# Hybrid decoder step on one core: the pooling, S5-gate and up-projection stages of the kernel written as one stage

## The chip, the core and the metric

The kernel runs on one core of a Trainium2 chip. The number that counts is the time of one execution in microseconds (us), as the device reports it; a kernel's figure is the median of its runs. The engines are TensorE (PE, its weight loads PEld), VectorE (DVE), ScalarE (ACT), GpSimd (POOL) and SyncE (SP, which here only starts transfers).

## The reference

One layer of a decoder trunk over 1024 prompt rows and 64 sample rows (1088 columns of work, `NT`). After RMSNorm and one input projection, three branches run side by side and are merged. What the change touches is the end of the layer:

```python
# S5 branch: y is the state-space output, w_glu is 512 x 512
y = jax.nn.gelu(y.reshape(bt, t, S5_W))
y = y * jax.nn.sigmoid(y @ w_glu)
# pooling branch: trailing means over 2, 4, 8, 16 rows, one 128-channel group each
outs.append((end - beg) / cnt)
pooled = jnp.concatenate(outs, axis=-1) - uf
mixed = jnp.einsum('btgc,gcd->btgd', pooled, pool_w) * pool_scale
# every branch: SiLU gate path, projection 512 -> 1024, sigmoid merge gate
u_s5 = (y_s5 * jax.nn.silu(s5_z)) @ w_up_s5
u_rw = (y_rw * jax.nn.silu(rw_z)) @ w_up_rwkv
u_pl = (y_pl * jax.nn.silu(pl_z)) @ w_up_pool
merged = gates[:, :, 0] * u_s5 + gates[:, :, 1] * u_rw + gates[:, :, 2] * u_pl
out = merged @ w_o
x = x + rmsnorm(out, g_post)
```

The last rows of the branches (shift row, pooling rows, RWKV state) are outputs too.

## The kernel before

All data are float32. A product that must be exact to float32 is made of three fp32r products (`split_mm`, lines 311 to 313): each operand is split into a high part (an ACT copy) and a low part (operand minus high part, on POOL or DVE). `CH` cuts the 1088 columns into chunks of 384, 384 and 320; `WB` = 4 is the number of 128-channel blocks of a branch, `KT` = 8 that of the model width. Activations lie as channels by columns. The order of work on each engine is the order in which its block of the program is written, and engines wait for one another by semaphores. Between two stages all engines meet at a barrier. All transfers are started by SP, in its program order.

Earlier stages (norm, input projection, RWKV) leave the projected columns in a DRAM tensor `projected`, the RWKV result in `y_branches`, and the S5 output in `s5_y_chunks`. Then come four stages:

- **Pooling** (`phase_pool`): SP loads all four pooling blocks, the tails and the pooling gate. PE turns the tails round (transposes, L1811 to L1824), ACT copies them out (L1839 to L1845), SP stores them. DVE makes doubling sums over all blocks at once (L1885, L1886), a pooled block per window (L1889 to L1894); PE multiplies it by a 128x128 weight in plain float32 (L1834), DVE scales and gates it (L1877). The result goes to DRAM (`y_branches`, L1803), and the stage ends when it has landed.
- **S5 gate** (`phase_glu`): SP loads the S5 output in eight pieces of 16 partitions (L1943), then the gate weight and the S5 gate path (L1944, L1945), then, for RWKV and pooling, a block's branch output and gate path (L1938, L1940) through three buffers. ACT does GELU (L2002) and SiLU (L2006), PE 48 plain float32 products (L2039), ACT their sigmoids (L2019). The table `order` (L1928) puts RWKV and pooling blocks ahead of and between the S5 blocks: SiLU (L2012), product on DVE (L1956), high part on ACT (L1999), low part on POOL (L1984).
- **Up projections** (`phase_up`): 24 units, for each of eight output blocks the three branches in turn; a unit is 36 fp32r matmuls over three chunks, in six PSUM banks. Per unit SP loads a weight and a merge gate (two buffers each), ACT splits the weight (L2087) and takes the gate's sigmoid (L2089), POOL makes the weight's low part (L2112), DVE multiplies a chunk by its gate and adds it to one accumulator (L2151, L2156). After every third unit the accumulator is split by ACT (L2096) and POOL (L2106) into `merged_hi` and `merged_lo`. The units are a loop of three rounds of six after a first six.
- **Output** (`phase_out`): the `w_o` product, the norm and the residual.

Of the kernel before, what the change touches and what calls it, by code (L numbers as in the profile page):

```python
# [19 lines left out]
ALU = mybir.AluOpType  # L20
# [1737 lines left out]
def phase_pool(nc, io, e):  # L1758

    EX = BUF + SEQ  # L1760
    ES_ = BUF + NS
    with ExitStack() as ctx:
        sem = lambda n: ctx.enter_context(nc.semaphore(n))
        sb = lambda n, s, d=F32: ctx.enter_context(nc.sbuf_tensor(n, s, d))
        ux, usx = sb("pool_ext", [P, WB, EX])[:, :, :], sb("pool_ext_s", [P, WB, NB, ES_])[:, :, :, :]
        fresh = sb("pool_fresh", [P, WB, NB * NS])
        old = sb("pool_old", [NB * BUF, W])
        pw = sb("pool_weights", [P, WB, P])

        sums = [sb(f"pool_sum{i}", [P, WB, EX]) for i in range(2)]  # L1770
        ssums = [sb(f"pool_ssum{i}", [P, WB, NB, ES_]) for i in range(2)]
        inv = sb("pool_inv", [P, WB, BUF])
        pooled = sb("pooled", [P, WB, NT])
        y_pl, z_pl = sb("y_pl", [P, WB, NT]), sb("z_pl", [P, WB, NT])
        z_loaded, z_silu = sem("pl_z_loaded"), sem("pl_z_silu")
        tail = sb("shift_tail", [P, RB, 1 + NB * NS])
        tail9 = sb("shift_cols", [P, RB, 1 + NB])
        shift_rows = sb("shift_rows_new", [1 + NB, RB * P])
        tail_p, tail_s = sb("pool_tail", [P, WB, BUF]), sb("pool_tail_s", [P, WB, NB * BUF])
        rows_p, rows_s = sb("pool_rows", [BUF, W]), sb("pool_rows_s", [NB * BUF, W])  # L1780
        st_rows = sb("rwkv_rows", [HD, H, HD])
        ps = [ctx.enter_context(nc.psum_tensor(f"pool_ps{i}", [P, 512], F32)) for i in range(8)]
        loaded, stored = sem("pl_loaded"), sem("pl_stored")
        flip, tails, done, mm_done, chain = [sem(n) for n in ("pl_flip", "pl_tails", "pooled_done", "pl_mm", "pl_chain")]
        flip2, rows_done, scaled = sem("pl_flip2"), sem("pl_rows"), sem("pl_scaled")
        scr = lambda b0, k, a, b: e.scratch[b0:b0 + k, :, a:b].rearrange("b p t -> p b t")
        with nc.Block() as block:
            @block.sync
            def _(sp):
                sp.dma_start(ux[:, :, BUF:EX], scr(B_PLX, WB, 1, 1 + SEQ)).then_inc(loaded, 16)  # L1790
                sp.dma_start(fresh[:, :, :], scr(B_PLX, WB, 1 + SEQ, 1 + NT)).then_inc(loaded, 16)
                sp.dma_start(old[:, :], io["state_pool"][0].rearrange("b t w -> (b t) w")).then_inc(loaded, 16)
                sp.dma_start(pw[:, :, :], io["pool_w"][0].rearrange("g c d -> c g d")).then_inc(loaded, 16)
                sp.dma_start(tail[:, :, :], scr(B_RW, RB, SEQ, 1 + NT)).then_inc(loaded, 16)
                sp.dma_start(z_pl[:, :, :], scr(B_PLZ, WB, 1, 1 + NT)).then_inc(z_loaded, 16)
                sp.wait_ge(rows_done, 7)
# [5 lines left out]
                sp.wait_ge(scaled, 3 * WB)  # L1802
                sp.dma_start(e.y_scr[2], y_pl[:, :, :]).then_inc(stored, 16)  # L1803
                sp.wait_ge(stored, 16 * 6)

            @block.tensor
            def _(pe):
                pe.wait_ge(loaded, 16 * 5)

                for b in range(WB):  # L1810
                    mm = pe.transpose(ps[0][:, b * NB * BUF:(b + 1) * NB * BUF], old[:, b * P:(b + 1) * P], e.ident[0:NB * BUF, 0:NB * BUF])  # L1811
                mm.then_inc(flip, 1)

                for b in range(WB):
                    mm = pe.transpose(ps[1][0:HD, b * P:(b + 1) * P], e.s_a[:, b, :], e.ident)
                mm.then_inc(flip2, 1)
                pe.wait_ge(tails, 3)
                for r in range(RB):
                    mm = pe.transpose(ps[2 + r // 4][0:1 + NB, (r % 4) * P:(r % 4 + 1) * P], tail9[:, r, :], e.ident)
                mm.then_inc(flip2, 1)  # L1820
                for b in range(WB):
                    mm = pe.transpose(ps[6][0:BUF, b * P:(b + 1) * P], tail_p[:, b, :], e.ident)
                for b in range(WB):
                    mm = pe.transpose(ps[7][0:NB * BUF, b * P:(b + 1) * P], tail_s[:, b, :], e.ident)  # L1824
                mm.then_inc(flip2, 1)
                for g in range(WB):
                    pe.wait_ge(done, g + 1)
                    for c, (at, n) in enumerate(CH):
                        q = g * 3 + c
                        if q == 0:  # L1830
                            pe.wait_ge(rows_done, 7)
                        if q >= 8:
                            pe.wait_ge(scaled, q - 7)
                        pe.matmul(ps[q % 8][:, 0:n], pw[:, g, :], pooled[:, g, at:at + n], start=True, stop=True).then_inc(mm_done, 1)  # L1834

            @block.scalar
            def _(act):
                act.wait_ge(flip2, 1)
                act.activation(st_rows[:, :, :], ps[1][0:HD, :].rearrange("v (h k) -> v h k", k=HD), ACT.Copy).then_inc(rows_done, 1)  # L1839
                act.wait_ge(flip2, 3)  # L1840
                for q in range(4):
                    n = min(4, RB - 4 * q) * P
                    act.activation(shift_rows[:, q * 512:q * 512 + n], ps[2 + q][0:1 + NB, 0:n], ACT.Copy).then_inc(rows_done, 1)
                act.activation(rows_p[:, :], ps[6][0:BUF, :], ACT.Copy).then_inc(rows_done, 1)
                act.activation(rows_s[:, :], ps[7][0:NB * BUF, :], ACT.Copy).then_inc(rows_done, 1)  # L1845
                act.wait_ge(z_loaded, 16)
                for g in range(WB):
                    act.activation(z_pl[:, g, :], z_pl[:, g, :], ACT.Silu).then_inc(z_silu, 1)

            @block.vector  # L1850
            def _(dve):
                ch = Chain(dve, chain)
                tt = dve.tensor_tensor
                ch.after(dve.memset(ux[:, :, 0:BUF], 0.0))

# [6 lines left out]
                dve.wait_ge(loaded, 16 * 5)  # L1862
                dve.tensor_copy(tail9[:, :, :], tail[:, :, 0:1 + NB * NS:NS]).then_inc(tails, 1)
                dve.tensor_copy(tail_p[:, :, :], ux[:, :, SEQ:EX]).then_inc(tails, 1)
                dve.wait_ge(flip, 1)
                ch.after(dve.tensor_copy(usx[:, :, :, 0:BUF], ps[0][:, 0:WB * NB * BUF].rearrange("p (w b t) -> p w b t", w=WB, b=NB)))
# [536 lines left out]
```

## Time and profile before

| | us |
|---|---|
| median of 3 runs (lowest, highest) | 1542.83 (1541.0, 1543.42) |
| profiled execution, its own time | 1539.99 |
| its span, first to last instruction | 1538.3 |
| PE, PEld busy | 1337.4, 1218.6 (87%, 79%) |
| DVE, ACT, POOL busy | 711.5, 480.1, 415.1 |
| mean granted TensorE clock | 0.935 |

The profile is of one execution. The busy sums say that TensorE works through most of the span; the 40 slices of the page show where it does not: in the slices from about 1115 to 1270 us PE is at 2 to 4 tenths, and the granted clock at 6 or 7 tenths of full speed. Those are the pooling and the S5-gate stage. The time outside the span is 1539.99 - 1538.3 = 1.69 us.

### The profile page before, as it was taken

To read this page: it belongs to the slowest core of one execution; us is meant where nothing else is said; L and a number is where in the kernel's file an instruction comes from. 1 tells how busy PE (TensorE), PEld (TensorE's weight loads), DVE (VectorE), ACT (ScalarE), POOL (GpSimd) and SP (SyncE) were. 2 spreads that over 40 slices of the span, in tenths; PEclk is the share of its full clock that TensorE was granted. 3 is DMA by queue.
4 is the path that set the end of the run, shared out by engine and by line. 5 is a ranking of instruction groups with operands and counts; after the bars stand their busy time and mean duration, and the time that the engine had idled before them with its cause. 6 is when DMAs were issued, how large, how long until landed. Compare 5 with 4: busy or idle time off the path is not lost. (4 is left out here: it accounts for less than half of the span.)

```text
span 1538.3 us, 32479 instructions
## 1 busy us (share of the span) xinstructions
PE 1337.4 (87%) x14048; PEld 1218.6 (79%) x14048; DVE 711.5 (46%) x1480; ACT 480.1 (31%) x851; POOL 415.1 (27%) x426
## 2 busy tenths in 40 slices
PE   3898999995799999999999999999823449997897
PEld 3897999995689889999988989899721239997785
DVE  5347724523637372827272737362315254444032
ACT  6121122121325242425252424252102443332221
POOL 6116457451112222222222221211000142332400
PEclk7898999998899999999999999999966679999899
DMA  5341422234222222222222222211063924442432
GB/s 180 78 114 34 120 90 86 69 105 117 51 62 70 76 65 81 65 76 70 76 65 82 64 80 61 70 53 57 21 180 92 231 87 143 142 128 83 146 137 69
DMA packets 158889, 141.33 MB, mean 92 GB/s; under 512 B 32096, under 2 KB 143761, under 8 KB 158625
## 3 DMA queue, kind: packets, MB, share of 16 engines
q1 hardware_dynamic: 158752, 139.33, 31.2%
q8 instruction: 107, 1.75, 0.5%
q14 instruction: 30, 0.24, 0.1%
HBM read 93.56 MB, written 44.57 MB: 90 GB/s over the span
## 5 line engine op out<-in xcount | busy, mean ns | idle before, releaser
L311 PE MATMUL f_ps<-h_hi,fw_hi 128*128 128x384 f32 (+1 forms) x864 | 305.2, 353 | 0.0
L313 PE MATMUL f_ps<-h_hi,fw_lo 128*128 128x384 f32 (+1 forms) x864 | 282.7, 327 | 0.0
L312 PE MATMUL f_ps<-h_lo,fw_hi 128*128 128x384 f32 (+1 forms) x864 | 282.2, 327 | 0.0
L1107 POOL TENSOR_TENSOR fw_lo<-fw,fw_hi 128x1024 fp32r<-128x1024 f32 x36 | 86.4, 2400 | 558.6 <-ACT fw_hi L1142 558.6
L311 PEld LDWEIGHTS f_ps<-h_hi,fw_hi 128*128 128x128 f32 x864 | 162.5, 188 | 13.8 <-issue 4.1
L311 PE MATMUL proj_ps<-h_hi,whi 128*128 128x384 f32 (+1 forms) x504 | 170.9, 339 | 1.1 <-PEq L220 1.1
L312 PE MATMUL proj_ps<-h_lo,whi 128*128 128x384 f32 (+1 forms) x504 | 166.2, 330 | 0.0
L313 PE MATMUL proj_ps<-h_hi,wlo 128*128 128x384 f32 (+1 forms) x504 | 166.1, 330 | 0.0
L312 PEld LDWEIGHTS f_ps<-h_lo,fw_hi 128*128 128x128 f32 x864 | 162.9, 189 | 3.9 <-issue 3.8
L313 PEld LDWEIGHTS f_ps<-h_hi,fw_lo 128*128 128x128 f32 x864 | 162.7, 188 | 0.0
L1186 ACT ACTIVATE f_out<-f_ps 128x384 f32<-128x384 f32 (+1 forms) x108 | 50.8, 470 | 281.4 <-PE f_ps L313 281.4
L311 PE MATMUL up_ps<-branch_hi,up_w_hi 128*128 128x384 f32 (+1 forms) x288 | 95.4, 331 | 23.7 <-PEq L1931 20.5
L1381 DVE TENSOR_TENSOR t_m<-t_m,q 128x256 f32<-128x256 f32 (+1 forms) x66 | 27.6, 418 | 174.1 <-PE q L1539 174.0
L311 PEld LDWEIGHTS proj_ps<-h_hi,whi 128*128 128x128 f32 x504 | 96.3, 191 | 3.4 <-issue 1.7
L312 PEld LDWEIGHTS proj_ps<-h_lo,whi 128*128 128x128 f32 x504 | 96.4, 191 | 0.5
L313 PEld LDWEIGHTS proj_ps<-h_hi,wlo 128*128 128x128 f32 x504 | 96.2, 191 | 0.0
L313 PE MATMUL up_ps<-branch_hi,up_w_lo 128*128 128x384 f32 (+1 forms) x288 | 94.6, 328 | 0.0
L312 PE MATMUL up_ps<-branch_lo,up_w_hi 128*128 128x384 f32 (+1 forms) x288 | 94.5, 328 | 0.0
L311 PEld LDWEIGHTS up_ps<-branch_hi,up_w_hi 128*128 128x128 f32 x288 | 54.6, 189 | 26.0 <-issue 21.0
L678 POOL TENSOR_TENSOR wlo<-wst,whi 128x1024 fp32r<-128x1024 f32 x18 | 43.3, 2406 | 104.7 <-ACT whi L882 104.0
L311 PE MATMUL out_ps<-wo_hi,merged_hi 128*128 128x512 f32 (+1 forms) x144 | 57.5, 399 | 12.9 <-POOL wo_lo L2210 12.2
L1984 POOL TENSOR_TENSOR branch_lo<-up_y,branch_hi 128x1088 fp32r<-128x1088 f32 x8 | 21.4, 2689 | 161.1 <-ACT branch_hi L1999 161.1
(418 smaller groups left out, 2635.9 us busy)
## 6 DMA issues: line engine op xcount, KB each, us to landing
fw<-in_w_in_dram SPq DMA_DIRECT2D x36, 512.0 KB, 4.7
projected<-f_out SPq DMA_DIRECT2D x72, 192.0 KB, 2.0
up_gate<-projected SPq DMA_DIRECT2D x24, 544.0 KB, 3.8
wst<-in_w_in_dram SPq DMA_DIRECT2D x21, 512.0 KB, 5.7
projected<-proj_out SPq DMA_DIRECT2D x17, 544.5 KB, 3.1
raw<-projected SPq DMA_DIRECT2D x8, 838.5 KB, 7.7
projected<-f_out SPq DMA_DIRECT2D x36, 160.0 KB, 2.1
up_y<-y_branches SPq DMA_DIRECT2D x8, 544.0 KB, 4.3
```

The costliest lines, as they stand in the source:

```text
L311: pe.matmul(out, whi, xhi, start=first, stop=False)
L312: pe.matmul(out, whi, xlo, start=False, stop=False)
L313: return pe.matmul(out, wlo, xhi, start=False, stop=last)
L678: pool.tensor_tensor(wlo[:, n % R], wst[:, n % R], whi[:, n % R].bitcast(F32), ALU.subtract).then_inc(lo_done, 1)
L1107: pool.tensor_tensor(wlo[:, r], wst[:, r], whi[:, r].bitcast(F32), ALU.subtract).then_inc(fw_lo, 1)
L1186: act.activation(stage[:, u % 3, 0:n], fps[u % 2][:, 0:n], ACT.Copy).then_inc(f_free, 1)
L1381: tt(tm[rows, hs], tm[rows, hs], q4(TXB[q])[rows], ALU.subtract).then_inc(ev["tmn"], 1)
L1984: pool.tensor_tensor(e.yl[:, br, b], y[:, n % YB], e.yh[:, br, b].bitcast(F32), ALU.subtract).then_inc(lo, 1)
```

## The change

`phase_pool`, `phase_glu` and `phase_up` become one stage, `phase_end`, with no barrier and no DRAM round trip inside.

- The first loads: SP starts the S5 output, RWKV blocks 0 and 1, the first two up weights, the tails and pooling weights, a gate, RWKV blocks 2 and 3, a gate and two pooling blocks; ACT starts the gate weight and the S5 gate path itself, ahead of its first activation.
- The S5 gate goes block by block (m = 0 to 3): three sigmoids, then RWKV block m whole (SiLU, product, high and low part), then copies of the turned tails.
- The 24 units run branch by branch (RWKV, S5, pooling), written out, in four PSUM banks instead of six; the sums of all eight output blocks stay in an SBUF tensor `up_acc`, and each is split for the output stage in the third run (n >= 18).
- Pooling is cut into single blocks and put between units: its sums and pooled blocks on DVE, its 12 products on PE in the other four banks after units 1, 5, 9 and 12, its SiLU and high parts on ACT, its low parts on POOL. It reads 0.5 MB blocks through two buffers and never goes to DRAM.

```diff
-def phase_pool(nc, io, e):
+UPS = [(br, m) for br in (1, 0, 2) for m in range(KT)]
+def phase_end(nc, io, e):
...
+    UB = 4
+        acc = sb("up_acc", [P, KT * NT])
+        aux = ps[4:8]
...
             def _(sp):
+                def load_rwkv(b):
+                    if b >= 2:
+                        sp.wait_ge(r_lo, b - 1)
...
+                def load_gate(n):
+                    br, m = UPS[n]
+                    if n >= 2:
+                        sp.wait_ge(gated, 3 * (n - 1))
...
+                for n in range(2, n_up):
+                    load_w(n)
+                    load_gate(n)
+                    if n in (2, 3):
+                        load_pool_gate(n - 2)
+                    if n in (3, 6):
+                        load_pool(2 + n // 6)
+                    if n in (10, 11):
+                        load_pool_gate(n - 8)
...
             def _(act):
+                act.dma_start(w5[:, :, :], io["s5_w_glu"][0].rearrange("(k p) m -> p k m", p=P)).then_inc(w5_loaded, 16)
+                act.dma_start(u5, scr(B_S5Z, WB, 1, 1 + NT)).then_inc(z5_loaded, 16)
...
+                for m in range(WB):
+                    for c, (_, n) in enumerate(CH):
+                        q = m * 3 + c
+                        act.wait_ge(mm5, q + 1)
+                        if q >= 2:
+                            act.wait_ge(out5, q - 1)
+                        act.activation(gate5[:, q % 2, 0:n], aux[q % UB][:, 0:n], ACT.Sigmoid).then_inc(sig5, 1)
+                    act.wait_ge(yz_loaded[m % 2], 32 * (m // 2 + 1))
+                    act.activation(uz[:, m % 2], uz[:, m % 2], ACT.Silu).then_inc(r_silu, 1)
+                    if m < 2:
+                        split(m)
+                    rwkv_high(m)
+                    if m:
+                        act.wait_ge(flip, m)
+                        for q in ((0, 1, 2), (3, 4, 5), (6,))[m - 1]:
+                            take(q)
...
             def _(pe):
+                for m in range(WB):
+                    glu(m)
+                    if m:
+                        turn_tails(m - 1)
+                for n in range(n_up):
+                    up(n)
+                    if n == 1:
+                        pe.wait_ge(sig5, 12)
+                        pool_products(0)
+                    if n == 5:
+                        pool_products(1)
+                    if n == 9:
+                        pool_products(2)
+                    if n == 12:
+                        pool_products(3)
...
             def _(dve):
+                for n in range(n_up):
+                    if n == 0:
+                        level(0, 0)
+                        pool_block(0)
+                    up(n)
+                    if n == 1:
+                        level(1, 0)
+                        level(1, 1)
+                    if n == 2:
+                        pool_block(1)
+                        level(2, 0)
...
-        phase_pool(nc, io, e)
...
-            phase_glu(nc, io, e)
...
-            phase_up(nc, io, e)
+        phase_end(nc, io, e)
```

Where instructions stand, in program order. First SP's queue from the stage's first transfer (before: from the S5-gate stage; `glu_yc` and the first `end_early` are the S5 output, the pairs from `y_branches` and `projected` are RWKV or pooling blocks):

```order
L1943 DMA glu_yc<-s_y_chunks 16x32x136 x8
L1944 DMA glu_w<-in_s_w_glu_dram 128x4x512
L1945 DMA glu_u<-projected 128x4x1088
L1938 DMA up_y<-y_branches 128x1088
L1940 DMA up_z<-projected 128x1088
```

The same place of the changed kernel, where one tensor `end_early` holds the S5 buffers and the branch buffers:

```order
L1843 DMA end_early<-s_y_chunks 16x32x136 x8
L1818 DMA end_early<-y_branches 128x1088
L1819 DMA end_early<-projected 128x1088
L1818 DMA end_early<-y_branches 128x1088
L1819 DMA end_early<-projected 128x1088
L1834 DMA up_w<-in_w_up_rwkv_dram 128x4x128 x2
L1848 DMA up_acc<-projected 128x13x65
```

The gate weight (1 MB) and the S5 gate path (2.1 MB) have left SP's queue; they are the first two instructions on ACT.

ACT in the kernel before, from the first sigmoid of the S5 gate (`glu_gate`) on; `branch_hi` are the high parts:

```order
L2019 ACT_TABLE_LOAD
L2019 ACTIVATE glu_gate<-glu_ps 128x384 x2
L2019 ACTIVATE glu_gate<-glu_ps 128x320
L1999 ACTIVATE branch_hi<-up_y 128x1088
L2019 ACTIVATE glu_gate<-glu_ps 128x384 x2
L2019 ACTIVATE glu_gate<-glu_ps 128x320
```

And block m = 1 of the changed kernel, where L1935 is the SiLU of an RWKV block, L1883 a weight's high part and the last two rows copy turned tails:

```order
L1933 ACT_TABLE_LOAD
L1933 ACTIVATE glu_gate<-end_ps 128x384 x2
L1933 ACTIVATE glu_gate<-end_ps 128x320
L1935 ACT_TABLE_LOAD
L1935 ACTIVATE end_early<-end_early 128x1088
L1883 ACTIVATE up_w_hi<-up_w 128x512
L1891 ACTIVATE branch_hi<-end_early 128x1088
L1908 ACTIVATE up_acc<-end_ps 64x512
L1912 ACTIVATE up_acc<-end_ps 9x512 x2
```

Sigmoid and SiLU now take turns, and each turn has an ACT_TABLE_LOAD; before, one stood ahead of all sigmoids.

PE in the changed kernel, from the S5 gate's second block to its third (L2000 are the gate's products, the others transposes of tails; before, all 48 gate products stood in a row):

```order
L2000 MATMUL end_ps<-end_early,glu_w 128x384 x8
L2000 MATMUL end_ps<-end_early,glu_w 128x320 x4
L2012 MATMUL end_ps<-ident,pool_old 128x120 x4
L2015 MATMUL end_ps<-ident,s_a 64x128 x4
L2005 MATMUL end_ps<-ident,shift_cols 9x128 x8
L2000 MATMUL end_ps<-end_early,glu_w 128x384 x8
```

The transposes of the tails have moved from the pooling stage in between the gate's blocks.

## Rows read from the trace of the kernel before

**Rows 1.** Windows by stage: pooling, S5 gate, up projections, output; busy us and count per engine.
```profile
1135.07:1184.67 49.60, 20.18 (x53) 10.88 (x53) 28.22 (x61) 8.64 (x12) 0.00 (x0) 0.64 0.48 164
1184.67:1266.57 81.90, 31.45 (x96) 19.10 (x96) 29.89 (x24) 38.58 (x41) 24.51 (x10) 0.69 0.64 155
1266.57:1421.04 154.47, 145.98 (x864) 143.93 (x864) 64.57 (x120) 48.65 (x54) 49.43 (x30) 0.99 0.41 124
1421.04:1538.30 117.26, 101.31 (x432) 80.27 (x432) 26.32 (x45) 24.45 (x54) 18.96 (x8) 0.92 0.33 117
```
Columns: window, length; PE, PEld, DVE, ACT, POOL; then granted clock, DMA share, GB/s.

**Rows 2.** Timeline of SP: start us, duration us; first transfers of three stages.
```profile
1135.07 0.40 SPq L1790 DMA_DIRECT2D pool_ext<-projected  x1
...
1184.67 9.80 SPq L1943 DMA_DIRECT2D glu_yc<-s_y_chunks  x8
...
1421.04 23.70 SPq L2194 DMA_DIRECT2D wo<-in_w_o_dram  x8
```

**Rows 3.** Windows of 5 us in the S5-gate stage, columns as in rows 1.
```profile
1195.00:1200.00 5.00, 0.00 (x0) 0.00 (x0) 0.00 (x0) 0.00 (x0) 0.00 (x0) 0.50 1.24 116
...
1210.00:1215.00 5.00, 0.33 (x1) 0.36 (x2) 0.00 (x0) 4.98 (x4) 0.00 (x0) 0.50 1.03 413
```

**Rows 4.** Timeline of ACT in the S5-gate stage.
```profile
1206.28 8.25 ACT L2002 ACTIVATE glu_act<-glu_yc 128x1088 f32<-128x1088 f32 x4 [20.32 <-DMA glu_yc<-s_y_chunks]
1214.55 1.28 ACT L2006 ACT_TABLE_LOAD   x1
1215.84 4.11 ACT L2006 ACTIVATE glu_u<-glu_u 128x1088 f32<-128x1088 f32 x4
...
1235.48 0.87 ACT L2019 ACTIVATE glu_gate<-glu_ps 128x384 f32<-128x384 f32 x2
```

**Rows 5.** Timeline of PE: tails, pooling products, S5 gate, first units, last matmul.
```profile
1149.60 2.94 PE L1819 MATMUL pool_ps<-ident,shift_cols 128*9 128x128 f32 x13 [0.54 <-DVE pool_tail_s L1869]
...
1162.31 2.10 PE L1834 MATMUL pool_ps<-pooled,pool_weights 128*128 128x384 f32 x6 [1.68 <-DVEq L1897]
1168.36 3.99 PE L1834 MATMUL pool_ps<-pooled,pool_weights 128*128 128x384 f32 x6 [3.96 <-DVEq L1897]
...
1214.67 31.45 PE L2039 MATMUL glu_ps<-glu_act,glu_w 128*128 128x384 f32 x96 [37.54 <-ACT glu_act L2002]
1266.62 0.66 PE L311 MATMUL up_ps<-branch_hi,up_w_hi 128*128 128x384 f32 x1 [20.51 <-PEq L1931]
...
1274.08 0.34 PE L311 MATMUL up_ps<-branch_hi,up_w_hi 128*128 128x384 f32 x1
...
1280.02 0.34 PE L311 MATMUL up_ps<-branch_hi,up_w_hi 128*128 128x384 f32 x1
...
1415.51 0.31 PE L313 MATMUL up_ps<-branch_hi,up_w_lo 128*128 128x320 f32 x1
```

**Rows 6.** Groups by line and form, 1135 to 1290 us: busy us, mean ns, idle before.
```profile
L1984 POOL TENSOR_TENSOR branch_lo<-up_y,branch_hi 128x1088 fp32r<-128x1088 f32 x8 | 21.4, 2689 | 161.1 <-ACT branch_hi L1999 161.1
...
L1999 ACT ACTIVATE branch_hi<-up_y 128x1088 fp32r<-128x1088 f32 x8 | 8.7, 1101 | 6.4 <-DMA up_y<-y_branches 5.2 <-DVE up_y L1956 1.2
...
L1956 DVE TENSOR_TENSOR up_y<-up_y,up_z 128x1088 f32<-128x1088 f32 x4 | 6.5, 1637 | 6.2 <-ACT up_z L2012 6.2
...
L2012 ACT ACTIVATE up_z<-up_z 128x1088 f32<-128x1088 f32 x4 | 4.3, 1098 | 5.8 <-DMA up_z<-projected 5.8
...
L2112 POOL TENSOR_TENSOR up_w_lo<-up_w,up_w_hi 128x512 fp32r<-128x512 f32 x2 | 2.8, 1380 | 16.4 <-ACT up_w_hi L2087 16.4
...
L1843 ACT ACTIVATE shift_rows_new<-pool_ps 9x512 f32<-9x512 f32 x3 | 1.5, 576 | 4.4 <-PE pool_ps L1824 4.4
...
L1885 DVE TENSOR_TENSOR pool_sum<-pool_sum 128x1024 f32<-128x1024 f32 x1 | 1.2, 1216 | 0.0
```

**Rows 7.** Transfers by line, of the page: KB each, median us from issue to landing.
```profile
up_gate<-projected SPq DMA_DIRECT2D x24, 544.0 KB, 3.8
```

**Rows 8.** Waits in the up projections: us in total, times, longest.
```profile
DVE up_acc L2151 <- POOL merged_lo L2106: 28.7, 7, 4.1
```

More of the change, by code:

```diff
@@ L1781, in phase_pool, with part @@
[L1781 to L1785, printed above, removed]
+        at = [0]
+        def part(n, parts=P):
+            v = room[0:parts, at[0]:at[0] + n]
+            at[0] += n
+            return v
@@ L1806, in _ @@
             @block.tensor
             def _(pe):
[L1808 to L1817, printed above, removed]
@@ L1826, in _ @@
-                for g in range(WB):
-                    pe.wait_ge(done, g + 1)
-                    for c, (at, n) in enumerate(CH):
[L1829 to L1848, printed above, removed]
+                def glu(m):
+                    for c, (at, n) in enumerate(CH):
+                        q = m * 3 + c
+                        if q >= UB:
+                            pe.wait_ge(sig5, q - UB + 1)
+                        for k in range(WB):
+                            mm = pe.matmul(aux[q % UB][:, 0:n], w5[:, k, m * P:(m + 1) * P], act_y[:, k, at:at + n], start=k == 0, stop=k == WB - 1)
+                        mm.then_inc(mm5, 1)
@@ new lines, in _ @@
+                pe.wait_ge(w5_loaded, 16)
+                pe.wait_ge(gelu, WB)
+                for m in range(WB):
+                    glu(m)
[12 more added lines that the diff above has]
+                        pool_products(3)
@@ new lines, in up @@
+                def up(n):
+                    br, m = UPS[n]
+                    dve.wait_ge(sig, n + 1)
+                    for c, (at, w) in enumerate(CH):
+                        q = 3 * n + c
+                        dve.wait_ge(mm_done, q + 1)
+                        a = acc[:, m * NT + at:m * NT + at + w]
+                        if n == 4 and c == 0:
+                            dve.wait_ge(stored, 16 * 5)
+                        if br == UPS[0][0]:
+                            tt(a, ps[q % UB][:, 0:w], gate[:, n % 2, at:at + w], ALU.mult).then_inc(gated, 1)
+                            dve.wait_ge(gated, q + 1)
+                            dve.sem_inc(summed, 1)
+                        else:
+                            tt(gu[:, q % 2, 0:w], ps[q % UB][:, 0:w], gate[:, n % 2, at:at + w], ALU.mult).then_inc(gated, 1)
+                            dve.wait_ge(gated, q + 1)
+                            tt(a, a, gu[:, q % 2, 0:w], ALU.add).then_inc(summed, 1)
+                            dve.wait_ge(summed, q + 1)
@@ L1861, in _ @@
                     ch.after(dve.memset(inv[:, g0:WB, pos:pos + 1], 1.0 / (pos + 1)))
[L1862 to L1866, printed above, removed]
-                ch.after(dve.tensor_copy(usx[:, :, :, BUF:ES_], fresh[:, :, :].rearrange("p w (b t) -> p w b t", b=NB)))
```

575 lines of the change are left out of this document (285 added, 290 removed).

## The prediction

> **What bounds the kernel now.** I read the windows by stage first [rows 1]. Pooling and S5 gate last 49.60 + 81.90 = 131.5 us, and PE is busy in 51.6 of them, at a granted clock of 0.64 and 0.69; the up projections last 154.47 us with PE busy for 145.98, at 0.99. So the first two stages are chains of transfers and single operations, and the third is TensorE itself. Then the timelines of SP, ACT and PE [rows 2, 4, 5]: look at what each first operation of a stage waited for. ACT's GELU waited 20.32 us for the S5 output, PE's gate products 37.54 us for the GELU, PE's first up unit 20.51 us for the end of the gate stage. Nothing of the output stage changes (117.26 us [rows 1]). The change is therefore worth what it takes from the 1421.04 - 1135.07 = 285.97 us between the first transfer of pooling and the first of the output stage [rows 2]. I count t from 1135.07.
>
> **The first loads.** Before, GELU started 1206.28 - 1184.67 = 21.6 us after the S5 output's first transfer [rows 2, 4]; that transfer now starts at t = 0. Beside it ACT's queue starts the gate weight and the gate path, 1024 + 2176 KB by their shapes, 3.28 MB: 7.9 us at the 413 GB/s that large transfers reached [rows 3]. The trace has one queue only and does not show how two share. Bounds: 21.6 us if the new ones fit into gaps, 29.5 us if they add. The DMA share of 1.24 during the S5 output speaks for adding; its 116 GB/s beside 413 [rows 3] says that something other than the engines' rate holds it, and speaks for gaps. No row lies nearer to one end, so I take the middle, 25.6. The Trainium skill (DMA: Bandwidth & Descriptors, "Issuing engines are not separate DMA queues") says that SP's and ACT's transfers run on the same 16 engines, and that a second issuer saves only the time to issue. By that rule the loads add and everything below comes 3.9 us later; no run here shows it.
>
> GELU 8.25, a table load 1.28 and the S5 SiLU 4.11 follow as before [rows 4]: t = 39.2.
>
> **Four rounds of S5 block and RWKV block.** Before, RWKV blocks ran apart from the S5 blocks; now ACT's order ties them. A round on ACT: two table loads 2.56, three sigmoids 1.3 (0.87 for two [rows 4], a little less for the narrow third), SiLU 1.10, the wait for DVE's product 1.64 (the mean; one of its four ran long), high part 1.10 [rows 6]: 7.7 us, four times 30.8. Behind the wait for the product stand the next sigmoids, and for those PE waits, but only once it is four chunks (some 10 us) ahead, which it never is. Six of the seven copies of turned tails stand ahead of the last high part: 6 x 0.58 = 3.5 [rows 6]. The weight splits fall into the waits for the product: nothing; without that cover 0.6 each. PE's 48 gate products took 31.45 us [rows 5], 7.9 per round and so close to ACT's pace; the transposes now between them add some 6 (2.94 for thirteen [rows 5]). Setting PE's chunk ends beside ACT's sigmoids, ACT waits for a chunk in rounds 0 and 2 mostly; with hand-overs I put 4.0. Together 38.3: the last RWKV high part is done at t = 77.5.
>
> POOL then makes its low part, 2.69, and the first weight's, 1.38 [rows 6]; with 0.2 of hand-over PE starts the first unit at **t = 81.8**, where before it started at 1266.62 - 1135.07 = 131.5 [rows 5].
>
> What is hidden on the way: RWKV blocks 2 and 3 are loaded once POOL is done with blocks 0 and 1 (t about 52 and 60) and need some 5 us (3.8 for one 544 KB transfer [rows 7], and a second behind it); they are wanted at t = 63 and 72. The tails come after the S5 output and are wanted at about t = 50. SP then waits for all seven copies, and the loads of units 2 onward stand behind that wait; it ends near t = 78, unit 2 comes at 97. DVE has four S5 low parts and the first pooling block to do after its last product, and reaches unit 0 at about t = 91; PE has by then just filled its four banks. Each microsecond that one of these is late beyond that costs one.
>
> **The 24 units.** A unit takes 1280.02 - 1274.08 = 5.94 us [rows 5]: 142.6. The first took 1274.08 - 1266.62 = 7.46, 1.5 more, at the lower clock after an idle stretch of 20.51; PE is idle for some 9 us here too, and I keep the 1.5. The stage took 1415.82 - 1266.62 = 149.2 us, so 149.2 - 142.6 - 1.5 = 5.1 were waits. They come with the single accumulator, for which DVE waited 28.7 us in seven places [rows 8]; eight separate sums need no such wait. I take 0 and keep 5.1 as the bound. PE's queue gains twelve pooling products: three took 2.10 us in one place and 3.99 in another, where the clock was low [rows 5]; at full clock 4 x 2.1 = 8.4, bound 16.0. DVE's pooling work, worth about 24 operations of 1.22 [rows 6] or 29 us over the stage, and eight table loads around pooling's SiLU on ACT lie beside PE: DVE and ACT were busy for 64.57 and 48.65 of 154.47 us [rows 1], and four banks let PE run 8 us ahead. Nothing, then; rival two says when not. The output blocks' splits come one per unit in the third run, POOL's 2.7 and 1.4 [rows 6] within 5.94.
>
> Units together 142.6 + 1.5 + 8.4 = 152.5: the last matmul ends at t = 234.3. From there to the output stage the instructions are the same as before, 1421.04 - 1415.82 = 5.2 us [rows 2, 5]: t = 239.5.
>
> **Sum.** 285.97 - 239.5 = 46.5 us less: 1539.99 - 46.5 = 1493.5 in the profiled execution's own time. The median of the runs shown lies 1542.83 - 1539.99 = 2.84 above it, so I forecast **1496** for the median.
>
> **Rival one: a table load costs more than its row.** Nine stand on the path up to the first unit. If each held ACT for as long again, 9 x 1.3 = 11.7, of which the 4.0 of waits would absorb some, the kernel would take about 1504. The row speaks against it: the GELU ends at 1206.28 + 8.25 = 1214.53, the load runs from 1214.55 to 1215.83, the SiLU starts at 1215.84 [rows 4]. The Trainium skill (ScalarE: Activation LUTs, "What ACT_TABLE_LOAD costs") puts 1283 ns on the load and 1380 ns on a drain; the trace agrees with the first and shows nothing of the second here. Chance 0.08.
>
> **Rival two: the merge gates come late, which at its end is slower than before.** A gate of unit n is loaded into one of two buffers, and SP starts it when DVE is through unit n - 2. That loop is issue 0.4 [rows 2], landing 3.8 [rows 7], a sigmoid 1.1 (as a SiLU of that size [rows 6]), DVE's unit 3.2 (six of the 120 operations that took 64.57 us [rows 1]) and up to 2.9 of pooling between: 8.5 to 11.4 us per two units, beside PE's 11.9. In some ten units little room is left, and pooling's blocks and gates, 0.5 MB each and 1.3 us at 413 GB/s, go ahead of them on the same queue, which takes its transfers in order. At a landing of 6 us those ten units lose about 1 us each: 1506. At 10 us the mean loop is 0.4 + 10 + 1.1 + 4.4 = 15.9, all 24 units lose 2 us, and the time is 1496 + 47 = 1543; just beyond that the kernel is slower than before. For it speaks the queue's order; against it that all 24 gate loads had a median of 3.8 and that DMA was at 0.41 in that stage [rows 1, 7]. Chance 0.18, and 0.03 of it at or beyond the point where the gain is gone.
>
> **How the numbers follow.** The forecast has 0.74, rival one 0.08, rival two 0.18. Downward: the loads at 21.6 give 1492, a first unit without its 1.5 gives 1490.5, and the runs spread by 2 us: 1488. Upward: the loads at 29.5 give 1500, the old 5.1 us of waits 1505, pooling products at the lower clock (7.6 more) 1512; that takes in rival one and the milder part of rival two. Range 1488 to 1512. A measurement of this kernel tells about 0.2%, some 3 us, from no change: faster 0.97, same 0.01, slower 0.02.
>
> **What would show it.** In the changed profile GELU should start 21 to 30 us after the stage's first transfer; ACT should go from round to round in 8 to 11 us with PE never waiting for a bank; the first up matmul should start near 1217 us; units should follow one another at 5.94 us with four gaps of about 2 us for pooling products; the output stage should start near 1375 us and last 117 us. The forecast is wrong if PE waits for weights or banks between units, if ACT idles between a table load and its activation, if the sigmoid of the merge gates waits so long for its transfer that DVE lags, or if the granted clock in the units is below 0.99.

## The result and the profile after

| | before | after |
|---|---|---|
| median (4 runs each) | 1542.48 us | 1502.92 us |
| profiled execution, its own time | 1539.99 | 1502.76 |
| its stage(s) from the first transfer to the output stage | 285.97 | 243.66 |

The ratio is 0.9745, 95% interval 0.9728 to 0.9762: faster, and inside the forecast's range (1488 to 1512, likeliest 1496). Of the profiled difference of 37.2 us, 42.3 come from the stage, 1.0 from the output stage, and 6.0 go the other way in the stages ahead, which the change doesn't touch.

Windows of the changed kernel: first loads, GELU to first unit, units, tail, output stage (columns as in [rows 1]):

```profile
1141.10:1172.34 31.24, 0.00 (x0) 0.00 (x0) 0.52 (x20) 1.28 (x1) 0.00 (x0) 0.50 1.09 194
1172.34:1225.59 53.25, 34.03 (x125) 21.64 (x125) 18.08 (x24) 45.42 (x50) 11.20 (x6) 0.82 0.49 152
1225.59:1378.31 152.72, 152.71 (x888) 149.62 (x888) 123.55 (x170) 67.01 (x72) 62.80 (x34) 0.98 0.45 141
1378.31:1384.76 6.45, 0.00 (x0) 0.00 (x0) 2.23 (x3) 1.11 (x1) 3.31 (x2) 0.75 0.00 0
1384.76:1501.00 116.24, 100.28 (x432) 79.51 (x432) 26.33 (x45) 24.46 (x54) 19.02 (x8) 0.94 0.34 118
```

In the units TensorE now works through the whole window, so ahead of the output stage waiting time is left only in the first two rows and the tail. The timeline of ACT (start, duration; ACTq rows are transfers that ACT issues) against [rows 4]:

```profile
1141.11 0.42 ACTq L1918 DMA_DIRECT2D glu_w<-in_s_w_glu_dram  x1
1141.56 0.53 ACTq L1919 DMA_DIRECT2D end_early<-projected  x1
...
1172.34 8.25 ACT L1922 ACTIVATE end_early<-end_early 128x1088 f32<-128x1088 f32 x4 [28.94 <-DMA end_early<-s_y_chunks]
1180.61 1.28 ACT L1926 ACT_TABLE_LOAD   x1
1181.90 4.11 ACT L1926 ACTIVATE end_early<-end_early 128x1088 f32<-128x1088 f32 x4
...
1190.17 1.28 ACT L1935 ACT_TABLE_LOAD   x1
1191.46 1.11 ACT L1935 ACTIVATE end_early<-end_early 128x1088 f32<-128x1088 f32 x1
1192.48 0.61 ACT L1883 ACTIVATE up_w_hi<-up_w 128x512 fp32r<-128x512 f32 x1
1193.93 1.11 ACT L1891 ACTIVATE branch_hi<-end_early 128x1088 fp32r<-128x1088 f32 x1 [0.84 <-DVE end_early L2155]
```

GELU waited for the S5 output until 31.2 us after the first transfer, where before it took 21.6 [rows 2, 4]. Behind it ACT has only short waits: the table load at 1190.17 ends at 1191.45 and its SiLU starts at 1191.46. The windows of the first loads say why GELU was late (compare [rows 3]):

```profile
1140.00:1145.00 5.00, 0.00 (x0) 0.00 (x0) 0.52 (x20) 1.28 (x1) 0.00 (x0) 0.50 0.47 167
1145.00:1150.00 5.00, 0.00 (x0) 0.00 (x0) 0.00 (x0) 0.00 (x0) 0.00 (x0) 0.50 1.06 273
1150.00:1155.00 5.00, 0.00 (x0) 0.00 (x0) 0.00 (x0) 0.00 (x0) 0.00 (x0) 0.50 1.05 302
1155.00:1160.00 5.00, 0.00 (x0) 0.00 (x0) 0.00 (x0) 0.00 (x0) 0.00 (x0) 0.50 1.23 124
```

While ACT's 3.28 MB run, the DMA engines are busy throughout (share 1.05 to 1.06 from 1145 to 1155) and move up to 302 GB/s; behind them the rate falls to the 124 GB/s of the S5 output alone. ACT's second transfer landed 15.6 us after its issue, at 1157.2. By then some 4.0 MB had moved (5 us each at 167, 273 and 302 GB/s, 2.2 us at 124), so of the S5 output's 2.23 MB about 0.7: beside the others it got on at little more than a third of its own rate.

### The profile page after: what moved, and what is told of

Same layout as the page of the kernel before. It is cut to its first block and busy times, and to the rows that moved or that the text cites. A ratio compares the mean times of both kernels' runs of the same rounds, so it can differ in the third digit from the quotient of the medians.

```text
span 1501.0 us, 32233 instructions
## 1 busy us (share of the span) xinstructions
PE 1331.4 (89%) x14048; PEld 1219.5 (81%) x14048; DVE 733.8 (49%) x1491; ACT 499.2 (33%) x866; POOL 418.4 (28%) x426
## 3 DMA queue, kind: packets, MB, share of 16 engines
q10 hardware_dynamic: 1056, 3.28, 0.7%
## 5 line engine op out<-in xcount | busy, mean ns | idle before, releaser
L1107 POOL TENSOR_TENSOR fw_lo<-fw,fw_hi 128x1024 fp32r<-128x1024 f32 x36 | 86.1, 2392 | 558.9 <-ACT fw_hi L1142 558.9
L2000 PE MATMUL end_ps<-end_early,glu_w 128*128 128x384 f32 (+1 forms) x96 | 31.2, 485 | 54.9 <-ACT end_early L1922 54.9
L311 PE MATMUL end_ps<-branch_hi,up_w_hi 128*128 128x384 f32 (+1 forms) x192 | 64.4, 335 | 10.8 <-POOL up_w_lo L1968 10.8
L2000 PEld LDWEIGHTS end_ps<-end_early,glu_w 128*128 128x128 f32 x96 | 18.7, 198 | 66.3 <-issue 56.3
L311 PE MATMUL out_ps<-wo_hi,merged_hi 128*128 128x512 f32 (+1 forms) x144 | 57.1, 397 | 14.2 <-POOL wo_lo L2258 13.5
L312 PE MATMUL end_ps<-branch_lo,up_w_hi 128*128 128x384 f32 (+1 forms) x192 | 63.8, 332 | 0.0
L313 PE MATMUL end_ps<-branch_hi,up_w_lo 128*128 128x384 f32 (+1 forms) x192 | 63.7, 332 | 0.0
```

The costliest lines, as they stand in the source:

```text
L311: pe.matmul(out, whi, xhi, start=first, stop=False)
L312: pe.matmul(out, whi, xlo, start=False, stop=False)
L313: return pe.matmul(out, wlo, xhi, start=False, stop=last)
L1107: pool.tensor_tensor(wlo[:, r], wst[:, r], whi[:, r].bitcast(F32), ALU.subtract).then_inc(fw_lo, 1)
L2000: mm = pe.matmul(aux[q % UB][:, 0:n], w5[:, k, m * P:(m + 1) * P], act_y[:, k, at:at + n], start=k == 0, stop=k == WB - 1)
```

## The experiments

**The same kernel again.** No edit.

> The changed kernel once more, nothing edited. In its first profile the stage's first transfer was issued at 1141.10 us, before at 1135.07, although nothing ahead of it is edited. Theory (one execution differs from the next): 1502.9 us within 0.2%, and this profile's first transfer anywhere from 1134 to 1142; from the first transfer on the same as in the first profile: GELU 31 us behind it, first unit 84.5, last unit's end 237. Rival (the edit itself makes the earlier stages 6 us longer, by where its code or its tensors lie): first transfer at 1141 again within 1 us, in every profile of a kernel that contains the change.

1502.12 us, ratio 0.9737 [0.9713, 0.9761]; first transfer at 1138.45, GELU 31.2 us behind it, first unit at 86.1, last matmul at 239.4. So one execution differs from the next ahead of the stage, and by some 2 us within it: it lasted 245.88 us for 243.66. This profile's first transfer is already 2.65 us earlier than 1141.10, and a later kernel that contains the change (e3_sigmoid) had its own at 1133.21, which rules the rival out. About half of the microseconds lie where the granted clock changes, at the end of the last RWKV tile: windows of the changed kernel, then of e3_sigmoid.

```profile
1085.00:1090.00 5.00, 4.21 (x72) 3.35 (x70) 0.00 (x0) 0.60 (x1) 0.00 (x0) 0.80 0.01 3
1090.00:1095.00 5.00, 4.14 (x24) 3.97 (x24) 2.77 (x5) 0.59 (x1) 0.00 (x0) 0.50 0.00 0
1095.00:1100.00 5.00, 5.00 (x25) 5.00 (x24) 1.11 (x2) 0.49 (x1) 0.00 (x0) 0.68 0.11 41
```
```profile
1085.00:1090.00 5.00, 4.14 (x31) 3.22 (x30) 1.66 (x3) 0.59 (x1) 0.00 (x0) 0.75 0.00 0
1090.00:1095.00 5.00, 5.00 (x37) 4.81 (x36) 2.21 (x4) 0.62 (x2) 0.00 (x0) 1.00 0.11 41
1095.00:1100.00 5.00, 3.35 (x25) 1.49 (x23) 3.94 (x8) 0.94 (x2) 0.00 (x0) 1.00 0.09 33
```

In both, TensorE runs 128 small products (L1692, 3.91 us) and is then idle for 0.79 us, and the granted clock falls from the higher of its two levels (2.4 GHz) to the lower (1.2 GHz); in e3_sigmoid it is back within the first window, in the changed kernel it stays low for some ten us. The small products start at 1082.84 in the one profile and at 1079.37 in the other, still at the full clock: of the 7.9 us by which the two first transfers differ, 3.5 are older than this place, their source open, and 4.4 come behind it. The experiments below are therefore read from their stage's first transfer on, with some 2 us of doubt within the stage, and their medians with some 4 us of this in mind.

**S5's gate weight and z behind the S5 output, on SP.**

```diff
                     sp.dma_start(yc[GC * q:GC * q + GC], e.y5_scr.rearrange("(t c) (b q) j -> q c b t j", c=GC, q=8)[q]).then_inc(y5_loaded, 16)
+                sp.dma_start(w5[:, :, :], io["s5_w_glu"][0].rearrange("(k p) m -> p k m", p=P)).then_inc(w5_loaded, 16)
+                sp.dma_start(u5, scr(B_S5Z, WB, 1, 1 + NT)).then_inc(z5_loaded, 16)
...
-                act.dma_start(w5[:, :, :], io["s5_w_glu"][0].rearrange("(k p) m -> p k m", p=P)).then_inc(w5_loaded, 16)
-                act.dma_start(u5, scr(B_S5Z, WB, 1, 1 + NT)).then_inc(z5_loaded, 16)
```

> The S5 gate weights and z, 3.28 MB, are issued by SP right behind the eight transfers of S5's output and no longer by ScalarE's queue beside them. Theory (the two queues share the 16 DMA engines, which the output's 544-byte packets fill by themselves at 116 to 124 GB/s, so what ScalarE's queue moves delays the output by its own time): GELU 21.6 us (21 to 24) behind the first transfer instead of 31.2, gate weights and z landing under GELU's 8.25 us, everything behind GELU earlier by as much: about 9.6 us less than the changed kernel, 1493 us (1491 to 1496). Rival one (the output is slow here for another reason, such as the destination of 16 partitions or what the RWKV stage left to write): GELU still 28 us or more behind the first transfer, 1501 to 1504. Rival two (GELU comes early but z or the branch loads then come late): GELU at 22, a wait for z or a branch's load of 5 us or more behind it, 1497 to 1501.

1489.67 us, ratio 0.9656 [0.9632, 0.9680], 12 to 13 less than the change. Window of the first load and ACT's row:

```profile
1134.87:1156.80 21.93, 0.00 (x0) 0.00 (x0) 0.52 (x20) 1.28 (x1) 0.00 (x0) 0.50 1.13 120
```
```profile
1156.80 8.25 ACT L1922 ACTIVATE end_early<-end_early 128x1088 f32<-128x1088 f32 x4 [20.65 <-DMA end_early<-s_y_chunks]
1165.07 1.28 ACT L1926 ACT_TABLE_LOAD   x1
```

GELU came 9.3 us earlier behind the first transfer, no later wait took its place, and the stage lasted 236.55 us, for 243.66 and 245.88 in the two profiles of the change: 7.1 and 9.3 less. The theory holds; both rivals fall. The median lies under the 1491 to 1496 expected. The rest of the 12 to 13 lies ahead of the stage, where the first transfer was earlier (1134.87 for 1141.10 and 1138.45); whether it is more than chance isn't settled.

**Only the gate weight beside it.** Of the edit above, the lines of `u5` alone.

```diff
+                sp.dma_start(u5, scr(B_S5Z, WB, 1, 1 + NT)).then_inc(z5_loaded, 16)
...
-                act.dma_start(u5, scr(B_S5Z, WB, 1, 1 + NT)).then_inc(z5_loaded, 16)
```

> Only the S5 gate weights, 1.05 MB of the 3.28, stay on ScalarE's queue beside S5's output; z is issued by SP behind it. Theory (what the other queue moves delays the output by its own time, in proportion): GELU 21.9 + 9.3 x 1.05 / 3.28 = 24.9 us (24 to 26) behind the first transfer. Rival (it is enough that a second queue is busy when the output is issued): 28 or more. Rival (only the large z matters): 22.

GELU at 25.7 us (1492.37 us, one run): 3.75 us for 1.05 MB, where 3.28 MB cost 9.3. Roughly in proportion, then, at 2.8 to 3.6 us per MB.

**No table changes in the rounds.**

```diff
-                    act.activation(uz[:, m % 2], uz[:, m % 2], ACT.Silu).then_inc(r_silu, 1)
+                    act.activation(uz[:, m % 2], uz[:, m % 2], ACT.Sigmoid).then_inc(r_silu, 1)
```

> The four RWKV gates use a sigmoid in place of SiLU, so that the four rounds need no change of ScalarE's function table: eight loads of 1.28 us fewer (10.2 us of ScalarE's time between GELU and the first unit). The RWKV branch's values are thereby others. Theory (TensorE's gate products and transposes, 34 us without a gap over 0.6 us from 1180.7 to 1214.8, set the pace of the rounds as much as ScalarE does): only what lies behind the last gate product gets shorter, about 2.8 us, 1500 us (1498 to 1501.5). Rival (ScalarE's chain sets the pace, and each table load lies on it): 8 to 10 us less, 1493 to 1495.

1496.9 us (1493.92 to 1499.67), ratio 0.9711 [0.9686, 0.9736], between the ranges of theory and rival, so that the time alone decides nothing. The median is 5 to 6 lower than the change's, but its first transfer was 5 to 8 earlier; from GELU to the first unit it took 51.4 us, for 53.3 and 54.9 in the two profiles of the change: 1.9 to 3.5 less. ACT's timeline shows where the eight loads went:

```profile
1196.73 0.46 ACT L1933 ACTIVATE glu_gate<-end_ps 128x384 f32<-128x384 f32 x1
1198.38 0.49 ACT L1933 ACTIVATE glu_gate<-end_ps 128x384 f32<-128x384 f32 x1 [1.19 <-PE end_ps L2000]
1200.53 0.44 ACT L1933 ACTIVATE glu_gate<-end_ps 128x320 f32<-128x320 f32 x1 [1.66 <-PE end_ps L2000]
```

ACT now waits for PE's chunk before eight of the twelve sigmoids, 10.8 us in all; in the changed kernel it waits once, for 1.51. The 10.2 us of loads were beside PE's gate products, as the theory had it.

**What holds the S5 output at 120 GB/s.** Alone in front, its 2.23 MB hold GELU back for 21.9 us. Six kernels load it in other shapes, all but the first in e2_behind's order. First, runs of 2176 bytes instead of 544 (the scratch's order is changed), with ACT's transfers still beside it:

```diff
-    e.y5_scr = dram("s5_y_chunks", (P, G, J5))
+    e.y5_scr = dram("s5_y_chunks", (P, 8, WB, J5))
...
-                    sp.dma_start(yc[GC * q:GC * q + GC], e.y5_scr.rearrange("(t c) (b q) j -> q c b t j", c=GC, q=8)[q]).then_inc(y5_loaded, 16)
+                    sp.dma_start(yc[GC * q:GC * q + GC], e.y5_scr.rearrange("(t c) q b j -> q c t b j", c=GC)[q]).then_inc(y5_loaded, 16)
```

> S5's output lies in its scratch with the four branch blocks of one row behind each other, so that its load moves 2176-byte runs in place of 544-byte ones; the S5 stage's stores are cut into 544-byte runs for it. The gate weights and z stay on ScalarE's queue. Theory (what fills the DMA engines in the output's load is its number of packets, 4096): 2.23 MB at 300 to 413 GB/s with 3.28 MB beside it, GELU 15 to 18 us behind the first transfer instead of 31.2, and 13 to 16 us less in all: 1487 to 1490 us, with the S5 stage as long as before. Rival one (the output's load is bound by its destination, 16 partitions per transfer): GELU at 30 or later, 1501 to 1504. Rival two (the stores in small runs make the S5 stage late): GELU at 15 to 18, but the first transfer itself later by 3 us or more.

1502.83 us (1495.1 to 1504.27), GELU at 30.2: my theory, the number of packets, falls. Then the same alone in front (this edit and that of e2_behind), and with 16 transfers to 8 partitions that lie 16 apart:

```diff
-                    sp.dma_start(yc[GC * q:GC * q + GC], e.y5_scr.rearrange("(t c) q b j -> q c t b j", c=GC)[q]).then_inc(y5_loaded, 16)
+                    sp.dma_start(yc[c:P:GC], e.y5_scr.rearrange("(t c) q b j -> c q t b j", c=GC)[c]).then_inc(y5_loaded, 16)
```

> The 2176-byte runs of e4_wide and the order of e2_behind together, so that S5's output is loaded by itself, still by eight transfers to 16 neighbouring partitions each. With 544-byte runs and alone it came 21.9 us behind the first transfer (120 GB/s). Theory one (the number of packets is the limit; in e4_wide the other queue hid that): GELU 9 to 13 us behind the first transfer, 9 to 13 us less than e2_behind in all, 1477 to 1481 us. Theory two (the limit lies at one end of the transfer, the 16 neighbouring partitions that are written or the rows that are read, whatever the size of the runs): GELU 20 to 23 behind it, the same as e2_behind within 2 us, 1488 to 1492.

> As e5_wide_behind, but S5's output is loaded by 16 transfers that each write 8 partitions that lie 16 apart, where it was eight transfers to 16 neighbouring ones; the same runs of 2176 bytes. Theory two, at the written end (neighbouring partitions share a way in): GELU 8 to 13 us behind the first transfer, 1477 to 1481 us, while e5_wide_behind stays at 21. Theory two, at the read end (the rows of the scratch): both at 20 to 23. Theory one (the number of packets): both at 9 to 13.

1489.83 us with GELU at 19.9, and 1492.88 us with GELU at 27.9. The first says that a quarter of the packets brings GELU 2 us forward in one profile and leaves the median where e2_behind's was (1489.67); the second fits none of the theories, and showed a DMA share of only 0.34 to 0.60 in its first 12 us. Counted in the trace, the packets in flight were 8 or 9 at the median of these 12 us, where they are 14 to 20 in e2_behind and e5_wide_behind, so that probably half of the engines had no work; the trace doesn't name them. Eight transfers over all 128 partitions, one run to each, showed the same low share:

```diff
-                    sp.dma_start(yc[GC * q:GC * q + GC], e.y5_scr.rearrange("(t c) q b j -> q c t b j", c=GC)[q]).then_inc(y5_loaded, 16)
+                    sp.dma_start(yc[:, t], e.y5_scr.rearrange("(t c) q b j -> t q c (b j)", c=GC)[t]).then_inc(y5_loaded, 16)
```

> As e5_wide_behind (S5's output alone in front, 2176-byte runs), but each of its eight transfers now writes 128 partitions, one run to each, where it wrote 16 partitions with eight runs to each; the same bytes, the same runs, the same rows read. Theory (few partitions at a time limit the transfer: 16 neighbouring ones gave 120 GB/s, 8 spread ones 79 to 114): near the 400 to 413 GB/s that the loads behind it reach, GELU 7 to 10 us behind the first transfer instead of 19.9 to 21.9, and 11 to 14 us less than e2_behind, 1476 to 1479 us. Rival one (the read end limits it, since the rows and runs are unchanged): GELU at 18 to 22, 1487 to 1491. Rival two (GELU comes early but the gate weights, z or the branch loads do not): GELU at 7 to 10, a wait of 4 us or more for a transfer behind it, 1481 to 1486.

1486.79 us, ratio 0.9646 [0.9621, 0.9671], GELU at 18.6 (21.8 in e12_best, with the same load), where the theory had 7 to 10. Its first three windows of 4 us:

```profile
1135.97:1139.97 4.00, 0.00 (x0) 0.00 (x0) 0.52 (x20) 1.28 (x1) 0.00 (x0) 0.50 0.31 89
1139.97:1143.97 4.00, 0.00 (x0) 0.00 (x0) 0.00 (x0) 0.00 (x0) 0.00 (x0) 0.50 0.66 214
1143.97:1147.97 4.00, 0.00 (x0) 0.00 (x0) 0.00 (x0) 0.00 (x0) 0.00 (x0) 0.50 1.06 249
```

Its read pattern has an outer dimension of eight, as e8_wide_spread's transfers have eight partitions. At two thirds of the share it moved 214 GB/s, more than 16 partitions did at the full one. But it was not alone for long: by the rates of its windows some 3.8 MB had moved by GELU, 1.5 more than the S5 output, because the gate weight and z queued behind it ran beside its rest (e8_wide_spread: 1.5 more too). How much of its 18.6 us that costs isn't shown. The last two kernels take one thing away each: the strided reading, with 16 neighbouring partitions kept, and both the eight and the 16.

```diff
-                    sp.dma_start(yc[GC * q:GC * q + GC], e.y5_scr.rearrange("(t c) (b q) j -> q c b t j", c=GC, q=8)[q]).then_inc(y5_loaded, 16)
+                    sp.dma_start(yc[GC * q:GC * q + GC], e.y5_scr[GC * q:GC * q + GC].rearrange("p (b t) j -> p b t j", t=L5)).then_inc(y5_loaded, 16)
```

> As e2_behind, but S5's output is loaded without its change of order: each of the eight transfers still writes 16 neighbouring partitions, and reads 16 whole rows of 17,408 bytes for them, so that the branch's values are others. Theory (writing 16 neighbouring partitions at a time is the limit): GELU 18 to 22 us behind the first transfer, as with runs of 544 and of 2176 bytes, and 1487 to 1491 us. Rival (it is the strided reading or the runs): GELU at 8 to 12, 1476 to 1481.

```diff
-    e.y5_scr = dram("s5_y_chunks", (P, G, J5))
+    e.y5_scr = dram("s5_y_chunks", (L5, P, WB, J5))
...
-                    sp.dma_start(e.y5_scr[:, groups(b)], ycut[:, :, :]).then_inc(y_st, 16)
+                    for t in range(L):
+                        sp.dma_start(e.y5_scr[t].rearrange("(q c) b j -> b c q j", c=GC)[b], ycut[GC * t:GC * t + GC, :, :]).then_inc(y_st, 16)
...
+                for t in range(L5):
+                    sp.dma_start(yc[:, t], e.y5_scr[t]).then_inc(y5_loaded, 16)
```

> As e12_best, but the scratch of S5's output lies in the order in which it is loaded, so that each of the eight transfers reads 128 whole rows of 2176 bytes one behind the other and writes one to each of 128 partitions (in e11_full and e12_best the same eight transfers showed only half of the DMA engines busy, share 0.31 to 0.66 in their first 8 us). The S5 stage's four stores become 32, each from 16 partitions. Theory (few engines or few partitions at a time limit the load): all engines busy, 300 to 413 GB/s, GELU 8 to 11 us behind the first transfer, 10 to 12 us less than e12_best, 1474 to 1478 us. Rival one (something else limits what is read from this scratch, such as where it lies): GELU at 18 to 22, 1485 to 1489. Rival two (32 stores instead of four, or stores from 16 partitions, hold up SP in the S5 stage): GELU at 8 to 11, but the first transfer later by 5 us or more.

Windows from the first transfer to GELU, of e14_straight and of e13_rows:

```profile
1131.67:1152.06 20.39, 0.00 (x0) 0.00 (x0) 0.52 (x20) 1.29 (x2) 0.00 (x0) 0.50 0.97 128
```
```profile
1138.11:1146.43 8.32, 0.00 (x0) 0.00 (x0) 0.52 (x20) 1.29 (x2) 0.00 (x0) 0.50 0.89 296
```

Whole rows of 17,408 bytes to 16 neighbouring partitions still took 20.4 us (1482.95 us in one run, under the 1487 to 1491 expected, with its first transfer at 1131.67), so neither the runs (544, 2176, 17,408 bytes: 21.9, 19.9, 20.4 us) nor the order of reading is the limit: writing 16 neighbouring partitions at a time is what the three have in common. With 128 partitions and the engines busy (0.89) GELU came at 8.3 us, and e13_rows ran in **1479.3 us**, ratio 0.9597 [0.9574, 0.9621]: the best of both kernels and of all experiments. Against e12_best it gained 7.2 us of the 13.5 by which GELU came earlier; its first transfer was at 1138.11 instead of 1133.97, with the clock at half from 1085 to 1095, so the rest is at least in part the stages ahead. The 32 stores have some share: the last of them lands at 372.7 us, where the last of four lands at 370.8 in e12_best, and of the 4.1 us by which the first transfers differ about 1 arises there. Only the order of the scratch, with its stores, differs from e12_best, so reading in that order is what filled the engines; that 16 partitions are a limit of their own rests on e2_behind, e5_wide_behind and e14_straight beside the 214 GB/s above.

**Two shorter waits**, on top of e2_behind: the weight's split ahead of the last RWKV low part, and the last merged blocks in chunks.

```diff
                 for b in range(WB):
...
-                split(0)
+                    if b == 2:
+                        split(0)
...
-                merged_high(n_up - 1)
+                for c, (at, w) in enumerate(CH):
+                    act.wait_ge(summed, 3 * (n_up - 1) + c + 1)
+                    act.activation(e.m_hi[:, KT - 1, at:at + w], acc[:, (KT - 1) * NT + at:(KT - 1) * NT + at + w], ACT.Copy).then_inc(m_hi, 1)
```

> As e2_behind, with two waits behind GELU shortened: GpSimd splits the first up weights ahead of the last RWKV low part instead of behind it (1.25 us), and the last two merged blocks are split into high and low parts in chunks, so that behind the last matmul only a chunk of 320 columns goes through ScalarE and GpSimd and no long GpSimd instruction meets VectorE's last additions (6.9 us now; estimate 0.5 + 0.5 + 0.5 + 0.8 and the hand-overs, 3.5 to 4.5). Theory (both lie on the path): 3.5 to 4.5 us less than e2_behind, 1485 to 1486.5 us. Rival (the clock at the first up unit or the output stage's first load takes it back): within 1 us of e2_behind.

> The edits of e11_full and e9_split_tail together. Theory (they lie one behind the other on the path): e11_full less 1.5 to 2 us, what e9_split_tail gave against e2_behind (0.5 ahead of the first unit, 1.4 in the tail); 1474 to 1477.5 us if e11_full comes as its theory says. Rival (within the spread of the stages ahead): no difference from e11_full that its interval shows.

1488.11 us [0.9628, 0.9672] and 1486.51 us [0.9612, 0.9664]: below their partners by 1.6 and 0.3, which the intervals don't tell from nothing. The profile of the first shows 0.5 us ahead of the first unit and a tail of 5.5 for 6.9, less than I had expected of both. In e12_best the tail is 5.3 for 7.3, but the load in front took 3.2 us longer than in e11_full, so the two times say nothing of the waits.

## Why the prediction was right, step by step

**First loads: the term that was mis-sized.** I took 25.6, the middle between gaps and adding (bounds 21.6 and 29.5); the profile had 31.2, above both and outside the 21 to 30 that was to show the forecast right. The upper bound priced 3.28 MB at the 413 GB/s of [rows 3], a rate reached there behind the S5 output; beside it the sum of the two queues was 273 to 302. The runs show adding: e2_behind and e10_w5_beside put it at 9.3 and 3.75 us, the first more than the bound's 7.9. The Trainium skill (DMA: Bandwidth & Descriptors, "Issuing engines are not separate DMA queues") says that transfers started by different engines run on the same 16 DMA engines; that was the better guide than the middle. The sentence that 116 GB/s "speaks for gaps" failed: the share of 1.24 in the same row already said that the engines had no gap, whatever held them.

**GELU to the first unit: 53.3 for 56.2.** GELU, load and SiLU took 13.7, as said; the rounds ran from 1186.03 to the last high part's end at 1221.76, 35.7 for 38.3. The product took 1.29 us each time, not 1.64: it never ran beside POOL, where the one long product of before, 2.69, ran beside POOL's subtraction. ACT's only visible wait for PE was 1.51, where I had put 4.0 with hand-overs. POOL's two operations took 3.8 for 4.3. e3_sigmoid shows what the text only touched: PE's pace was so near that ACT's loads were almost free. Rival one (0.08) is out: each load shows 1.28 us with its activation right behind.

**Units: 152.7 for 152.5.** First unit, and one place with pooling products, in PE's timeline:

```profile
1225.59 0.69 PE L311 MATMUL end_ps<-branch_hi,up_w_hi 128*128 128x384 f32 x1 [10.83 <-POOL up_w_lo L1968]
...
1240.18 1.99 PE L2039 MATMUL end_ps<-pooled,pool_weights 128*128 128x384 f32 x6
1241.76 0.58 PE L311 MATMUL end_ps<-branch_hi,up_w_hi 128*128 128x384 f32 x1
```

The sum came right by luck, from two errors: the granted clock stayed at the lower level for the first 17 matmuls, so that the first unit took 8.65, 2.7 more than 5.94 where I had kept 1.5; and a place with pooling products cost about 1.85 us (the remainder, 152.7 - 142.6 - 2.7 = 7.4 in four places) where I had 2.1. The clock of the units' window, 0.98, is under the 0.99 that the forecast named as a sign of being wrong; it comes from the first unit alone (0.67, and 1.00 behind it). The waits were 0, as taken. PE's waits in the whole stage, and the transfer of the merge gates:

```profile
PE end_ps L2000 <- ACT end_early L1922: 54.9, 1, 54.9
PE end_ps L311 <- POOL up_w_lo L1968: 10.8, 1, 10.8
```
```profile
up_gate<-projected SPq DMA_DIRECT2D x24, 544.0 KB, 3.7
```

No wait of PE between units: rival two (0.18) is out, its landing of 3.7 us being that of before [rows 7].

**Tail: 6.45 for 5.2.** I took it over from before as unchanged; now the block ahead is still being split when the last chunks are added. DVE, POOL and ACT behind the last unit's first chunk:

```profile
1376.62 2.53 POOL L1973 TENSOR_TENSOR merged_lo<-up_acc,merged_hi 128x1088 fp32r<-128x1088 f32 x1 [1.57 <-ACT merged_hi L1904]
1376.66 0.56 DVE L2138 TENSOR_TENSOR up_gu<-end_ps,up_gate 128x384 f32<-128x384 f32 x1
1377.25 2.31 DVE L2140 TENSOR_TENSOR up_acc<-up_acc,up_gu 128x384 f32<-128x384 f32 x1
...
1380.65 1.11 ACT L1904 ACTIVATE merged_hi<-up_acc 128x1088 fp32r<-128x1088 f32 x1 [4.11 <-DVE up_acc L2140]
```

An addition that elsewhere takes 0.56 us took 2.31 beside POOL's subtraction, and ended 0.4 behind it. The whole profile bears this out: of the 48 additions of that line (L2140), the 28 that started while no POOL subtraction ran took 0.49 to 0.56 us, and each of the other 20 ended 0.34 to 0.42 us behind the subtraction, however long that still ran; the longest took 2.85 us.

**The balance.** 5.6 - 3.0 + 0.2 + 1.25 = 4.1 us: 239.5 forecast, 243.66 measured. The other 2.8 of the 6.9 us between 1496 and 1502.92 lie outside the stage, in what the forecast left unchanged: 6.0 from the later first transfer, less 1.0 of the output stage, less 2.7 because the median lies 0.16 above the profiled execution and not 2.84; rounding is the rest. So the mechanism was right, with the first loads as the term that was too small, and the nearness of the number owes something to errors that offset one another.

## What to carry to other kernels

A second issuing queue doesn't bring a late transfer forward where the engines are already busy: put what is needed first alone in front, and let the rest land under the work that it starts. Before counting packets of a slow load, look at how many partitions each transfer writes and at the DMA share: a low rate at a full share, and a low rate at half a share, want different cures. And before costing an engine's operations on a path, set its pace beside the engine that it waits for; what is shorter than the gap to the next one gains nothing.

## What was not expected of the hardware

- Loads that write 16 neighbouring partitions per transfer ran at 120 to 128 GB/s with the DMA engines shown as busy (share 0.97 to 1.13), with runs of 544 to 17,408 bytes; 128 partitions, one row each, ran at 296 over the same stretch, issue and landing included.
- A load whose transfers have eight partitions, or eight as the outer dimension of what they read, showed the DMA engines busy by a third to two thirds (0.31 to 0.66) in its first 8 to 12 us, with half as many packets in flight, and the loads queued behind it ran beside its rest. GELU came at 18.6, 21.8 and 27.9 us, for 19.9 with 16 neighbouring partitions.
- A DVE addition that starts while POOL's subtraction runs ends 0.34 to 0.42 us behind it, in 20 of 20 cases of one profile; alone it takes 0.49 to 0.56.
- At the end of the RWKV stage the same products and idle time were followed by nothing to some ten us at the lower clock, differently from one execution to the next, and in some profiles by a second such stretch. In 14 profiles the stage's first transfer came between 1131.00 and 1141.10 us, though the kernels are alike up to there but for the S5 stores of six. The clock explains a part of it: from 1085 to 1115 it had not fallen at all at 1131.67 and was low for 14 us at 1141.10, but for 17 at 1139.27 (e4_wide), and the 128 small products ahead already start anywhere from 1077.14 to 1082.84, at the full clock.
